# Opening matmuls on zeros in twelve narrow pieces, and key transposes that wait head by head

## The chip, the cores and the metric

The kernel runs on one core of a Trainium2 chip. The metric is the device time of one execution in microseconds; lower is better. A core has TensorE (PE; its weight loads are listed apart as PEld), VectorE (DVE), ScalarE (ACT), GpSimd (POOL) and the queue engine SyncE (SP). They run side by side and wait for each other by semaphores.

## The reference, cut to what matters

One step of a decoder with two layers, for a prompt of 256 tokens and 64 sample tokens (320 columns in all), width 1024. The first layer is retention (projections, a decayed score matrix, a state per head, an output projection), then one shared key and value pair is computed, then a block-sparse attention layer reads it. The changed code touches two things: the very start, and the normalised keys.

```python
def shared_kv(x, kv_norm_w, w_kv, k_norm_w):
    kv = rmsnorm(x, kv_norm_w) @ w_kv
    k, v = jnp.split(kv, 2, axis=-1)
    k = rmsnorm(k.reshape(B, T, MOBA_HEADS, MOBA_HD), k_norm_w)   # per head
    ...
```

The keys leave the kernel as rows (tokens by features), and are used inside it as columns (features by tokens), hence the transposes.

## The kernel before

All work is one hand-written list of steps, `make_schedule()`. Every engine runs through the same list and emits its own share of each step, so the order on each engine is fixed by the list, and semaphores join them. Weights come in chunks of 1 MB. ACT makes a rounded copy `w_hi` (L1239), DVE the remainder `w_lo` (L1579), and PE runs each projection as three matmuls, hi by hi, hi by lo, lo by hi (L940 with 320 moving columns, L937 with 512; the stacked sample tile is L921). A chunk is split in four parts during the chunk before it, at steps `WS`.

**The start.** PE waits for POOL's `eps_done`, then runs three matmuls of zeros (L956, tile `qz`) into bank 7, whose result nobody reads. Then it transposes the norm weights (L959, needed by ACT's `wcols`, L1312) and the inputs block by block (L877): eight blocks of the first 128 tokens, four of the second, four of the samples, and the rest when it has landed. DVE copies banks 0 and 1 to `xT` (L1633), ACT scales the others into `xn_hi` (L1323), DVE makes `xn_lo` (L1628), and the first projection begins.

**The keys.** The keys come in two halves of four heads (`mk` with h = 0 and 1), each in three token tiles in the order samples, first 128, second 128 (`tile_order`: 2, 0, 1). For each tile ACT squares the sums (L1407), DVE reduces and scales (L1737, L1742, L1747), and step `KN` on ACT multiplies the four heads of the tile by their root (L1504, four instructions of 128 columns, each some 0.3 us behind the last). `KN` signals `rows_done` once per tile. Steps `KX` 0 to 3 on PE transpose two heads each: three tiles by two heads is six transposes (L1126), head i into bank 6 + i. ACT then copies the two banks to `mkT` (L1511). `KX` 0 and 2 come first after the last tile of their half, `KX` 1 and 3 follow six projection matmuls later. Behind `KX` 1 six matmuls and then step `KS` 2 follow on PE: 64 calls of narrow key scores (L1111). An f32 matmul call is two matmuls and two weight loads on PE, so this pass is 256 instructions; a transpose is one of each. Also behind it, ACT cannot write the next half's sample rows (L1226) before the rows of the first half are stored (`rows_stored`, issued at L846 on SP) and before PE's tile at L921 is full.

Of the kernel before, what the change touches and what calls it, by code (L numbers as in the profile page):

```python
# [30 lines left out]
ACT = mybir.ActivationFunctionType  # L31
AX = mybir.AxisListType

P = 128
# [112 lines left out]
def tile_order(kind, a, b):  # L147

    return (2, 0, 1) if kind == "mk" or (kind, a, b) == ("mo", 1, 1) else tuple(range(TILES[kind]))
# [171 lines left out]
def build(nc, a):  # L321
# [3 lines left out]
    with ctx:  # L325
# [209 lines left out]
        def await_free(pe, b, *key):  # L535

            if use[(*key, b)]:
                pe.wait_ge(bank_read[b], use[(*key, b)])
# [140 lines left out]
        def _(sp):  # L679
# [77 lines left out]
            for step in steps:  # L757
# [65 lines left out]
                elif kind == "US":  # L823
                    store_pair(4 * step[1] + 3)
                    load_pair(4 * step[1] + 6)
                elif kind == "ME" and 1 <= step[1] < MH - 1:
                    if step[1] == 1:
                        sp.wait_ge(pages_loaded, 16)
                        await_ret_over(sp)
                        sp.dma_start(knw[:, :], bass.AP(a["k_norm_w"].tensor, 0, [[0, P], [1, HD]])).then_inc(knw_loaded, 16)  # L830
                    for n in ((), (0, 1), (2,), (3,), (4,), (5, 6), (7,))[step[1]]:
                        load_page(n)
                elif kind == "KP":
                    for n, at in ORDERED_AT.items():
                        if at == step[1]:
                            load_page(n)
                elif kind == "SE" and step[1] == 1:
                    await_ks(sp, 3)
                    sp.dma_start(tb[:, :, :], bass.AP(scratch.tensor, FAR - P, [[skew, P], [LINE, MH], [1, TP]]))\
                        .then_inc(tb_loaded, 16)  # L840
                elif kind == "KX" and step[1] % 2 == 0:
                    p = step[1] // 2
                    for n, t in enumerate(tile_order("mk", p, 1)):
                        m = TOK[t][1]
                        sp.wait_ge(rows_done, 3 * p + n + 1)
                        sp.dma_start(k_out[t][:, 512 * p:512 * p + 512], rows[0:m, t, :]).then_inc(rows_stored, 16)  # L846
                elif kind == "SN":
                    load_page(16 + NCP - 1)
                elif kind == "PV" and 1 <= step[1] <= 16 - NCP:
                    load_page(15 + NCP + step[1])  # L850
                elif kind == "YA" and step[1] == 0:
                    for t in range(3):
                        await_read(sp, *tile_use("mv", 3 + t))
                    for t, (c0, m) in enumerate(TOK):
                        store(v_out[t], mvp[:, t, :] if t < 2 else mvs[0:TS, :])
                elif kind == "TILE" and chunks[step[1]][0] == "mo":
                    p, t = chunks[step[1]][1], step[2]
                    await_read(sp, *tile_use("mo", 3 * p + t))
                    sp.dma_start(y_out[t][:, 512 * p:512 * p + 512], rows[0:TOK[t][1], t, :]).then_inc(rows_stored, 16)
# [8 lines left out]
        def _(pe):  # L868
            def close(mm, b):
                mm.then_inc(bank_full[b], 1)  # L870
# [80 lines left out]
            for step in steps:  # L951
                kind = step[0]
                if kind == "X":
                    pe.wait_ge(eps_done, 1)
                    for n in range(3):
                        pe.matmul(bank[7][:, 0:TP], qz[:, 0:P], qz[:, 0:TP], start=True, stop=True)  # L956
                    pe.wait_ge(eye_loaded, 16)
                    pe.wait_ge(ret_w_loaded, 16)
                    pe.transpose(bank[3][:, 384:392], wrow[0:8, :], ident[0:8, 0:8]).then_inc(wrow_turned, 1)  # L959
# [158 lines left out]
                        last[3].then_inc(ks_done, 1)  # L1118
                elif kind == "KX":
                    c = step[1]  # L1120
                    pe.wait_ge(rows_done, 3 * (c // 2) + 3)
                    def key_columns(i, t):

                        c0 = TOK[t][0]
                        at = 256 * (c % 2) + P * i
                        return pe.transpose(bank[6 + i][:, c0:c0 + P], rows[:, t, at:at + P], ident)  # L1126

                    if c == 0:
                        pe.wait_ge(pads_cleared, 1)
                    for i in range(2):  # L1130
                        await_free(pe, 6 + i, *step)
                        key_columns(i, 0)
                        key_columns(i, 1)
                    for i in range(2):
                        close(key_columns(i, 2), 6 + i)
                elif kind == "SN":
                    await_free(pe, 4, *step)
                    await_read(pe, 6, "KX", 3)
# [82 lines left out]
        def _(act):  # L1221
# [27 lines left out]
            for step in steps:  # L1249
# [248 lines left out]
                elif kind == "KN":  # L1498
# [2 lines left out]
                    m = TOK[t][1]  # L1501
                    await_read(act, *tile_use("mk", 3 * (n // 3) + t))
                    for d in range(4):
                        ins = act.activation(rows[0:m, t, P * d:P * d + P], rows[0:m, t, P * d:P * d + P], ACT.Copy,  # L1504
                                             scale=kss[0:m, n % 2, d:d + 1])
                    ins.then_inc(rows_done, 1)
                elif kind == "KX":
                    act.wait_ge(kt_done, 6)
                    for i in range(2):
# [60 lines left out]
        def _(dve):  # L1570
# [48 lines left out]
            for step in steps:  # L1619
# [74 lines left out]
                elif kind == "TILE":  # L1694
# [33 lines left out]
                    elif what == "mk":  # L1728
# [4 lines left out]
                            upper_half(rows[0:TS, i, :], b).then_inc(sum_done, 1)  # L1733
                        dve.wait_ge(key_sq_done, nk + 1)
                        if nk >= 2:
                            dve.wait_ge(rows_done, nk - 1)
                        dve.tensor_reduce(kss[0:m, nk % 2, :], key_sq[0:m, :].rearrange("p (h d) -> p h d", d=HD), AX.X, ALU.add)\  # L1737
                            .then_inc(key_sum_done, 1)
                        if h:
# [365 lines left out]
```

## Time and profile before

| what | value |
|---|---|
| time, median of 3 runs | 501.35 us (500.54 to 501.76) |
| the profiled execution, its own time | 499.29 us |
| its span, first to last instruction | 497.4 us |
| PE busy | 489.1 us (98%) |
| weight loads busy | 423.8 us (85%) |
| DVE, ACT, POOL busy | 359.0, 260.7, 96.5 us |

PE is busy almost everywhere, so an instruction more on PE costs its time unless PE would have waited there anyway. A matmul's duration in the trace reaches from its start to the end of its passage, and the next one starts before that; what it costs in a stream is the distance from start to start.

### The profile page before, as it was taken

Reading aid. Unit: us, or ns where it says so; the run is one execution under the profiler, and the core shown is the slowest. Engines: PE = TensorE matmul, PEld = TensorE weight load, DVE = VectorE, ACT = ScalarE, POOL = GpSimd, SP = SyncE. Lnnn points to the kernel's source line nnn. Section 1 sums busy time; section 2 is a strip of 40 time slices with the busy share of each in tenths; the row PEclk is TensorE's granted clock in tenths of the full one; section 3 lists DMA queues with packets and bytes.
Section 4 is the critical chain, followed back from the end, with each engine's and each line's share of the span. In section 5 each row is a group of like instructions: output and inputs, shape, how many; then the busy total and the mean of one; then the engine's idle time right before and its main releaser. Section 6 shows DMA issues by size and latency. Waiting matters only on the chain.

```text
span 497.4 us, 9895 instructions
## 1 busy us (share of the span) xinstructions
PE 489.1 (98%) x3685; PEld 423.8 (85%) x3685; DVE 359.0 (72%) x633; ACT 260.7 (52%) x536; POOL 96.5 (19%) x139
## 2 busy tenths in 40 slices
PE   7999999999999999999999999999989999999997
PEld 6889978899788997799799999987757778999885
DVE  3865539894698829896389987998966764775662
ACT  6735533565417724375454364764737655556630
POOL 0291003720063200920000042446002000000000
PEclk9999999999999999999999999999999999999999
DMA  9993978999899998999956899989798477683211
GB/s 264 368 330 118 278 252 304 371 367 238 266 333 394 261 233 300 348 361 238 261 169 211 294 298 224 280 224 220 239 298 281 154 229 234 232 307 124 86 53 53
DMA packets 86770, 125.54 MB, mean 252 GB/s; under 512 B 5491, under 2 KB 51524, under 8 KB 86596
## 3 DMA queue, kind: packets, MB, share of 16 engines
q1 hardware_dynamic: 85874, 124.63, 80.6%
q8 instruction: 29, 0.48, 0.4%
q0 software_dynamic: 768, 0.28, 0.4%
q14 instruction: 17, 0.14, 0.1%
q10 hardware_dynamic: 82, 0.02, 0.0%
HBM read 98.93 MB, written 27.57 MB: 254 GB/s over the span
## 4 chain that ended last, share of the span: by engine, by line
PE 88%; DVE 3%; DMA 3%; ACT 2%; issue 1%; SPq 1%; DVEq 0%; ACTq 0%
PE bank L940 44%; PE bank L937 18%; PE bank L921 7%; PE bank L1049 3%; DMA w_raw<-in_ret_w_in 3%; PE bank L1169 2%; PE bank L1063 1%; PE bank L996 1%; PE bank L1111 1%; PE bank L1215 1%; ACT rows L1504 1%; DVE small L1737 1%; PE bank L1029 1%; PE bank L1030 1%; PE bank L1031 1%
## 5 line engine op out<-in xcount | busy, mean ns | idle before, releaser
L1579 DVE TENSOR_TENSOR w_lo<-w_raw,w_hi 128x512 fp32r<-128x512 f32 x207 | 145.1, 739 | 62.8 <-ACT w_hi L1239 62.0
L1239 ACT ACTIVATE w_hi<-w_raw 128x512 fp32r<-128x512 f32 x208 | 118.6, 620 | 65.8 <-PE bank L940 35.4
L940 PE MATMUL bank<-xn_hi,w_hi 128*128 128x320 f32 x320 | 100.2, 317 | 0.2 <-DVE raw_qk L1669 0.2
L940 PE MATMUL bank<-xn_hi,w_lo 128*128 128x320 f32 x320 | 97.6, 309 | 0.0
L940 PE MATMUL bank<-xn_lo,w_hi 128*128 128x320 f32 x320 | 97.5, 309 | 0.0
L937 PE MATMUL bank<-w_hi,xn_hi 128*128 128x512 f32 x160 | 64.8, 405 | 0.0
L940 PEld LDWEIGHTS bank<-xn_hi,w_hi 128*128 128x128 f32 x320 | 59.7, 188 | 4.2 <-issue 2.7
L937 PE MATMUL bank<-w_lo,xn_hi 128*128 128x512 f32 x160 | 62.5, 391 | 0.0
L937 PE MATMUL bank<-w_hi,xn_lo 128*128 128x512 f32 x160 | 62.4, 390 | 0.0
L940 PE MATMUL bank<-ym_hi,w_hi 128*128 128x320 f32 x192 | 60.9, 317 | 0.0
L940 PEld LDWEIGHTS bank<-xn_lo,w_hi 128*128 128x128 f32 x320 | 59.8, 188 | 0.2
L940 PEld LDWEIGHTS bank<-xn_hi,w_lo 128*128 128x128 f32 x320 | 59.8, 188 | 0.0
L940 PE MATMUL bank<-ym_hi,w_lo 128*128 128x320 f32 x192 | 59.3, 309 | 0.0
L940 PE MATMUL bank<-ym_lo,w_hi 128*128 128x320 f32 x192 | 59.3, 309 | 0.0
L1798 DVE SCALAR_TENSOR_TENSOR st<-st,bank 128x512 f32<-128x512 f32 x64 | 39.6, 681 | 6.1 <-PE bank L1063 6.1
L2007 POOL TENSOR_TENSOR fin<-raw_qk,cst 128x320 f32<-128x320 f32 x16 | 17.4, 1109 | 109.8 <-DMA out_ret_state_prompt<-fin 101.5
L940 PEld LDWEIGHTS bank<-ym_hi,w_hi 128*128 128x128 f32 x192 | 36.1, 188 | 1.8 <-issue 1.7
L937 PEld LDWEIGHTS bank<-w_hi,xn_hi 128*128 128x128 f32 x160 | 30.0, 188 | 8.6 <-issue 3.1
L940 PEld LDWEIGHTS bank<-ym_lo,w_hi 128*128 128x128 f32 x192 | 36.1, 188 | 0.1
L940 PEld LDWEIGHTS bank<-ym_hi,w_lo 128*128 128x128 f32 x192 | 36.0, 188 | 0.0
L937 PEld LDWEIGHTS bank<-w_lo,xn_hi 128*128 128x128 f32 x160 | 30.0, 188 | 6.6
L937 PEld LDWEIGHTS bank<-w_hi,xn_lo 128*128 128x128 f32 x160 | 30.1, 188 | 5.6
(289 smaller groups left out, 780.1 us busy)
## 6 DMA issues: line engine op xcount, KB each, us to landing
w_raw<-in_ret_w_in SPq DMA_DIRECT2D x23, 1024.0 KB, 11.0
st<-in_state_ret SPq DMA_DIRECT2D x32, 512.0 KB, 8.2
out_ret_state_sample<-st SPq DMA_DIRECT2D x32, 512.0 KB, 4.6
w_raw<-in_ret_w_out SPq DMA_DIRECT2D x8, 1024.0 KB, 8.7
w_raw<-in_moba_w_in SPq DMA_DIRECT2D x8, 1024.0 KB, 6.5
w_raw<-in_w_kv SPq DMA_DIRECT2D x8, 1024.0 KB, 8.1
cache<-in_cache_v SPq DMA_DIRECT2D x16, 512.0 KB, 4.9
cache<-in_cache_k SPq DMA_DIRECT2D x44, 128.0 KB, 4.5
```

What stands on the lines that cost most here:

```text
L921: mm = pe.matmul(bank[b][:, :], xn_hi[:, k, TP:T + TS], w[:, wk, :], start=k == 0 and n == 0, stop=k == KT - 1 and n == 1)
L937: mm = pe.matmul(bank[b][0:m, :], x[:, k, c0:c0 + m], w[:, wk, :], **flags)
L940: mm = pe.matmul(bank[out][:, 0:T], w[:, wk, P * tile:P * tile + P], x[:, k, :], **flags)
L996: mm = pe.matmul(bank[5][0:m, col:col + n], kT[:, d, j:j + m], qT[:, d, i0:i0 + n], start=d == 0, stop=d == 1)
L1029: pe.matmul(bank[3 + d][:, :], kd_hi[:, t, at], vp_hi[:, t, :], start=t == 0, stop=False)
L1030: pe.matmul(bank[3 + d][:, :], kd_hi[:, t, at], vp_lo[:, t, :], start=False, stop=False)
L1049: mm = pe.matmul(bank[5][32 * j:32 * j + 32, :], qz[:, q0:q0 + 32], st[:, b, DV * d:DV * d + DV], start=False, stop=g == 1 and d == 1, ski ...
L1169: mm = pe.matmul(bank[7][32 * j:32 * j + 32, P * u:P * u + P], window(8 * half_at + 4 * (j // 2) + 2 * pg + j % 2, b % 4), page_at(16 + m) ...
L1239: act.activation(w_hi[:, c % 2, part], w_raw[:, c % RAW, part], ACT.Copy).then_inc(w_hi_done, 1)
L1579: dve.tensor_tensor(w_lo[:, c % 2, part], w_raw[:, c % RAW, part], w_hi[:, c % 2, part].bitcast(F32), ALU.subtract).then_inc(w_lo_done, 1)
L1798: dve.scalar_tensor_tensor(state, state, math.exp(NEW * LOG_DECAY[h]), bank[up_bank(b, d)][:, :], ALU.mult, ALU.add).then_inc(bank_read[up ...
L2007: done(pool.tensor_tensor(to, x, tab, ALU.mult))
```

## The change

The opening runs twelve matmuls of 64 columns in place of three of 256. Each call reloads the same 128 columns of weights. `KN` signals each head, so that all counts of `rows_done` are multiplied by four. `KX` takes the tiles in the order in which they become ready, and waits for the last tile head by head. The waits for banks 6 and 7 both stand ahead of the first tile.

```diff
-                    for n in range(3):
-                        pe.matmul(bank[7][:, 0:TP], qz[:, 0:P], qz[:, 0:TP], start=True, stop=True)
+                    for n in range(12):
+                        pe.matmul(bank[7][:, 0:TP // 4], qz[:, 0:P], qz[:, 0:TP // 4], start=True, stop=True)
...
-                    pe.wait_ge(rows_done, 3 * (c // 2) + 3)
...
-                    for i in range(2):
-                        await_free(pe, 6 + i, *step)
-                        key_columns(i, 0)
-                        key_columns(i, 1)
-                    for i in range(2):
-                        close(key_columns(i, 2), 6 + i)
+                    order = tile_order("mk", c // 2, 0)
+                    pe.wait_ge(rows_done, 4 * (3 * (c // 2) + 2))
+                    for n, t in enumerate(order):
+                        for i in range(2):
+                            if n == 0:
+                                await_free(pe, 6 + i, *step)
+                            if n == 2:
+                                pe.wait_ge(rows_done, 4 * (3 * (c // 2) + 2) + 2 * (c % 2) + i + 1)
+                            mm = key_columns(i, t)
+                            if n == 2:
+                                close(mm, 6 + i)
...
-                        ins = act.activation(rows[0:m, t, P * d:P * d + P], rows[0:m, t, P * d:P * d + P], ACT.Copy,
-                                             scale=kss[0:m, n % 2, d:d + 1])
-                    ins.then_inc(rows_done, 1)
+                        act.activation(rows[0:m, t, P * d:P * d + P], rows[0:m, t, P * d:P * d + P], ACT.Copy,
+                                       scale=kss[0:m, n % 2, d:d + 1]).then_inc(rows_done, 1)
```

The waits on `rows_done` of SP (before the stores of the rows) and of DVE (before it reuses `kss`) are multiplied by four likewise and stand for the same tiles.

PE's first rows before the change. `qz` is the tile of zeros, `st` holds the inputs, `fin` the norm weights.

```order
L867 UNCONDITIONAL_BRANCH [waits barrier_Pool_Activation_PE_DVE_SP_release]
L956 MATMUL bank<-qz 128x256 [waits eps_done]
L956 MATMUL bank<-qz 128x256 x2
L959 MATMUL bank<-eye,fin 128x8 [waits ret_w_loaded,eye_loaded]
L877 MATMUL bank<-eye,st 128x128 [waits x_loaded0]
```

The same rows of the changed kernel.

```order
L867 UNCONDITIONAL_BRANCH [waits barrier_Pool_Activation_PE_DVE_SP_release]
L956 MATMUL bank<-qz 128x64 [waits eps_done]
L956 MATMUL bank<-qz 128x64 x11
L959 MATMUL bank<-eye,fin 128x8 [waits ret_w_loaded,eye_loaded]
L877 MATMUL bank<-eye,st 128x128 [waits x_loaded0]
```

Nothing moved there; nine calls came in, which are 36 instructions of PE, and everything behind them stands 36 instructions later in PE's code.

PE's rows at `KX` 0 before the change (the projection of the second half's tile ends above it and goes on below it).

```order
L937 MATMUL bank<-w_lo,xn_hi 128x512
L1126 MATMUL bank<-eye,rows 128x128 [waits bank_read6,pads_cleared,rows_done]
L1126 MATMUL bank<-eye,rows 128x128
L1126 MATMUL bank<-eye,rows 128x128 [waits bank_read7]
L1126 MATMUL bank<-eye,rows 128x128 x3
```

The same place in the changed kernel.

```order
L937 MATMUL bank<-w_lo,xn_hi 128x512
L1125 MATMUL bank<-eye,rows 128x128 [waits bank_read6,rows_done,pads_cleared]
L1125 MATMUL bank<-eye,rows 128x128 [waits bank_read7]
L1125 MATMUL bank<-eye,rows 128x128 x2
L1125 MATMUL bank<-eye,rows 128x128 [waits rows_done] x2
```

The wait for the last tile moved from the first transpose to the fifth and sixth, and the wait for bank 7 from the third to the second. `KX` 1, 2 and 3 changed in the same way.

## Rows read from the trace of the kernel before

**Rows 1.** The page: busy time, granted clock in 40 slices, PE's code queue.
```profile
PE 489.1 (98%) x3685; PEld 423.8 (85%) x3685; DVE 359.0 (72%) x633; ACT 260.7 (52%) x536; POOL 96.5 (19%) x139
...
PEclk9999999999999999999999999999999999999999
...
q8 instruction: 29, 0.48, 0.4%
```

**Rows 2.** Weight loads by line: ns min/median/max, first and last start, forms.
```profile
L956 PEld LDWEIGHTS bank<-qz x6: 285/337/337, 1.7 to 3.5; 128*128 128x128 f32 x6
L877 PEld LDWEIGHTS bank<-eye,st x24: 134/140/230, 4.8 to 10.3; 128*128 128x128 f32 x16, 64*128 64x128 f32 x8
L970 PEld LDWEIGHTS bank<-gs,ones x6: 182/188/192, 18.5 to 19.3; 128*128 128x128 f32 x4, 64*128 64x128 f32 x2
```

**Rows 3.** Timeline of PE, first 20 us: start, us from first to last.
```profile
1.67 2.93 PE L956 MATMUL bank<-qz 128*128 128x256 f32 x6 [1.67 <-POOL eps L1964]
4.58 0.27 PE L959 MATMUL bank<-eye,fin 8*128 8x8 f32 x1
...
5.05 1.27 PE L877 MATMUL bank<-eye,st 128*128 128x128 f32 x5
...
6.54 0.64 PE L877 MATMUL bank<-eye,st 128*128 128x128 f32 x4
...
8.62 0.66 PE L877 MATMUL bank<-eye,st 128*128 128x128 f32 x4 [1.05 <-DMA st<-in_x_prompt]
...
18.66 0.61 PE L970 MATMUL bank<-gs,ones 128*128 128x128 f32 x4
...
19.20 0.43 PE L970 MATMUL bank<-gs,ones 64*128 64x64 f32 x2
```

**Rows 4.** Timeline of ACT and DVE between 7 and 10 us.
```profile
7.86 0.93 ACT L1323 ACTIVATE xn_hi<-bank,wcols 128x320 fp32r<-128x320 f32 x2
...
7.42 0.89 DVE L1633 COPY xT<-bank 128x320 f32<-128x320 f32 x2 [7.42 <-PE bank L877]
8.22 0.68 DVE L1579 TENSOR_TENSOR w_lo<-w_raw,w_hi 128x512 fp32r<-128x512 f32 x1
```

**Rows 5.** Timeline of PE from 21 to 23 us.
```profile
21.65 0.60 PE L1076 MATMUL bank<-fin 32*8 32x264 f32 x2
22.41 0.41 PE L940 MATMUL bank<-xn_hi,w_hi 128*128 128x320 f32 x1 [0.16 <-DVE raw_qk L1669]
```

**Rows 6.** One stretch: length; busy of PE, PEld, DVE, ACT, POOL; clock; DMA; GB/s.
```profile
22.40:355.90 333.50, 333.49 (x2321) 292.90 (x2321) 258.21 (x410) 169.84 (x317) 90.27 (x123) 1.00 0.91 275
```

**Rows 7.** Timeline of PE around the key transposes.
```profile
355.90 0.39 PE L937 MATMUL bank<-w_lo,xn_hi 128*128 128x512 f32 x1
356.56 0.87 PE L1126 MATMUL bank<-eye,rows 128*128 128x128 f32 x6 [0.27 <-ACT rows L1504]
...
358.65 0.82 PE L1126 MATMUL bank<-eye,rows 128*128 128x128 f32 x6
...
380.25 0.87 PE L1126 MATMUL bank<-eye,rows 128*128 128x128 f32 x6
```

**Rows 8.** Timeline of ACT in the same place.
```profile
355.22 1.28 ACT L1504 ACTIVATE rows<-rows,small 128x128 f32<-128x128 f32 x4 [0.51 <-DVE small L1747]
356.41 1.66 ACT L1239 ACTIVATE w_hi<-w_raw 128x512 fp32r<-128x512 f32 x3
357.97 0.74 ACT L1511 ACTIVATE mkT<-bank 128x320 f32<-128x320 f32 x2
```

**Rows 9.** Timeline of PE in the pass of key scores of step KS 2.
```profile
365.08 0.63 PE L1111 MATMUL bank<-scr,wide 32*32 32x256 f32 x8 [1.61 <-issue]
```

**Rows 10.** Stores of the key rows, and the ACT instruction that waits for them.
```profile
360.02 1.06 SPq L846 DMA_DIRECT2D out_k_prompt<-rows  x2
...
DMA to landing us min/median/max: 6.9/7.1/7.3
...
367.99 0.60 ACT L1226 ACTIVATE rows<-bank 64x512 f32<-64x512 f32 x1 [4.16 <-PE bank L921]
```

More of the change, by code:

```diff
@@ L844, in _ @@
                         m = TOK[t][1]
-                        sp.wait_ge(rows_done, 3 * p + n + 1)
+                        sp.wait_ge(rows_done, 4 * (3 * p + n + 1))
                         sp.dma_start(k_out[t][:, 512 * p:512 * p + 512], rows[0:m, t, :]).then_inc(rows_stored, 16)
@@ L1735, in _ @@
                         if nk >= 2:
-                            dve.wait_ge(rows_done, nk - 1)
+                            dve.wait_ge(rows_done, 4 * (nk - 1))
                         dve.tensor_reduce(kss[0:m, nk % 2, :], key_sq[0:m, :].rearrange("p (h d) -> p h d", d=HD), AX.X, ALU.add)\
```

## The prediction

> **What bounds the kernel now.** I read the page first: PE is busy 98% of the span and runs 3685 matmuls with as many weight loads [rows 1]. Then the timeline of PE for its idle times. There are five: before the opening [rows 3], 1.05 us for the inputs [rows 3], 0.16 us at 22.41 [rows 5], 0.27 us before a key transpose [rows 7], and 1.61 us inside a pass of key scores, ended by "issue", that is, by no semaphore [rows 9]. Between 22.4 and 355.9 us PE is never idle [rows 6]. So a delay that reaches 22.4 us arrives whole at 355.9; what happens before can be absorbed only by the waits for the inputs and at 22.41.
>
> **The opening.** Three calls are six matmuls with six weight loads, 2.93 us from the first start to the last end, some 0.43 us from start to start [rows 3]. Twelve calls are 24 of each. Streaming is a quarter of 0.43, 0.107 us a piece, and 24 × 0.107 = 2.6 us, as long as before. That is the lower bound. But each piece loads 128 columns of f32 weights. At the faster clock the trace has such loads with 128 moving columns, (0.61 - 0.275) / 3 = 0.11 us apart, and with 64, two that begin at 19.20 and are through about 0.27 us later, so 0.11 too, after a late first one [rows 3]. Half the columns save nothing: the load sets the pace. The durations say the same: a transpose's load lasts 140 ns, this one 188, and in the opening 337 against 230 at most [rows 2].
>
> The clock: the page prints full clock in every slice [rows 1], but equal transposes stand (1.27 - 0.42) / 4 = 0.21 us apart at 5.05 and (0.64 - 0.31) / 3 = 0.11 from 6.54 on [rows 3]. So PE is at 1.2 GHz until about 6.5 us and at 2.4 GHz after. At the lower level a load-bound piece takes twice 0.11, say 0.213 us. From an effective first start at 1.83, 24 × 0.213 = 5.1 us end at 6.9, not 4.4. Before, PE then stood until 4.58 for its first data [rows 3], and the input transposes ran from 4.84; now they run from 6.96, 2.1 us later.
>
> The Trainium skill ("TensorE: Matmul & The Clock Gate", LDWEIGHTS (loading the stationary operand)) gives a weight load as its columns divided by 1.2, in ns: 107 ns for these 128 columns. By that rule the pieces would stream at 0.107 us and the opening would cost nothing; the rows above, where 64 columns are no faster than 128, speak against it for f32.
>
> How much of 2.1 us is left? From 6.96 on, with the clock up: twelve at 0.109, a break of 0.1, four at about 0.06, done at 8.6 in place of 7.4. Just then the rest of the inputs has landed (8.62), so PE's idle 1.05 us is used up. But DVE's copies start with the sample blocks: 7.42 becomes 8.67; ACT's first scaling 7.86 becomes 8.8 [rows 4]. Behind the copies come DVE's weight split (0.68 us [rows 4]) and the first `xn_lo`, which the first projection's third term needs. It starts at 9.6 and stutters; I get the end of its first six matmuls 1.0 us later than before. From there PE streams without a gap to 21.87, and at 22.41 it had to wait: its last matmul at L1076 is streamed by 21.65 + 2 × 0.22 = 22.09, the next is effective at 22.5, held by DVE's `raw_qk`, which hangs on a weight transfer and not on PE. So 0.4 us are absorbed. Left: **+0.6 us**, taken as it is to 355.9.
>
> **The key transposes.** At KX 0 PE is free at 355.90 + 0.23 = 356.13 and starts effectively at 356.61, when the fourth head of ACT's row is done (355.22 + 1.28 = 356.50) [rows 7, 8]. KX 0 needs heads 0 and 1: at 0.3 us from head to head they are done at about 355.6 and 355.9. In the changed kernel nothing holds it: it ends 0.48 us earlier. But KX 1 needs bank 6 and 7 again, and these are freed by ACT's copies, which stand behind three weight splits: 356.41 to 358.07, then copies ending at about 358.39 and 358.71 [rows 8]. ACT is busy without a gap, so they don't come sooner. KX 1 started at 358.65 and came to its wait for bank 7 two transposes later, 0.05 us after it was free. Now it arrives at 358.17, does one transpose when bank 6 is free, and holds for bank 7 until 358.76: five more at 0.109, next matmul at about 359.37. Before it was 359.30. So the gain of 0.48 is given back wholly and 0.06 more, since the wait for bank 7 stands one transpose earlier. The second half has the same shape: KX 2 gains less, some 0.25 us, since its row names no wait [rows 7], and KX 3 meets the copies behind the same three splits; ends about 0.04 later. **+0.05 us** in all. Four signals in place of one on ACT cost nothing that I see: its instructions with a signal each, as the splits at 0.52 us apart, run gapless [rows 8].
>
> **The 36 instructions.** PE's code comes through a queue of its own: 29 packets, 0.48 MB [rows 1], so 16.5 KB or some 254 of PE's 7370 instructions each. PE is short of code when it runs through one block before the next has come. The pass at KS 2 is 256 instructions in under 3 us, and its stall lies 8 matmuls, 16 instructions, before its end [rows 9]: the block begins 16 before the pass and holds almost nothing but the pass, the worst alignment there is. The other three passes don't stall. Everything now stands 36 later, so the boundary falls 52 before the end of the pass, and the block before it begins near KX 0's first instruction and not within KX 1. The request goes out by about 355.8 and not at 358.65, when KX 1 began [rows 7]; if it takes as long as before (6.4 us, until 365.08), the code is there at 362.2, when it is wanted. The 1.6 us (1.8 with what a stream would have filled) vanish.
>
> The Trainium skill ("Runtime: NRT & Kernel Launch", Instruction fetch mechanics) speaks of blocks of 16 KiB, 256 instructions, whose boundary costs mostly nothing; the block size agrees with the packets, the stall of 1.61 us does not agree with the cost.
>
> What is late next? PE gets 1.8 us ahead, and at L1226 ACT waits for the stored rows of the first half: issued at 360.02 and about 360.6, landed 6.9 to 7.3 us later, so at 367.9; it starts at 367.99 [rows 10]. PE's tile was full at about 367.8, so the row names it, but the store alone holds ACT there. All that follows up to the next 380.21 (rows of the last tile, four heads) runs on ACT and DVE, one behind the other, and PE meets it at KX 2 and, after the splits, at KX 3. What PE is ahead, it waits there. **0 us**, bounds -1.8 (all kept) and +0.
>
> **Sum.** 499.29 + 0.6 + 0.05 + 0 = 499.9 for an execution like the profiled one. That lies 2.1 below the median of the runs shown; on the median, 501.35 + 0.65 = **502.0 us**.
>
> **The rivals.**
> *The clock rises later.* The opening now keeps the array streaming half the time, and what PE did before the rise is only shown for the wide one. If PE is at 1.2 GHz until about 10 us, twelve transposes at 0.213 end at 9.5, the samples at 10.1, the rest at 10.8; DVE's copies come 2.8 us late, and after the 0.4 at 22.4 some +2.3 remain: 503.7. For it: nothing shows the narrow form. Against: PE is not idle in it.
> *The opening costs nothing.* Loads hide behind 64 columns, or the clock is up by 5 us: +0.05, 501.4. Against it stand the L970 rows.
> *Faster: the stall's time is kept.* One mechanism: the rows' stores land before PE's tile is full, so that PE, not the store, releases L1226, and each 0.1 us of PE counts. It decides if they land by 366.2 rather than 367.9: then -1.8 + 0.65, 500.2. For it: the row names PE and the two are 0.15 us apart. Against: the stores' issue hangs on SP's page loads, which the change doesn't touch.
> *Another pass now runs out of code.* Boundaries move in all dense passes; the closest I find has 7 us. Up to +2: 504.
>
> **How the numbers follow.** Chances: forecast 0.50 (its own range 501.4 to 502.8), late clock 0.17, free opening 0.15, stall kept 0.12, new stall 0.06. What a measurement tells from no change is 0.3%, 1.5 us. Faster by more needs the kept stall and a free opening together: 0.05. Slower by more is the late clock (most of it), the new stall and the forecast's edge: 0.18. The rest, 0.77, is within. The range goes from the kept stall to just short of the late clock's centre, 500.2 to 503.4, and leaves out under 0.2.
>
> **What would show it.** L956 as 24 matmuls over about 5 us and the first L877 near 6.8; DVE's L1633 near 8.7; the first L1511 after KX 0 still right behind three splits and KX 1 no earlier than before relative to it; no 1.6 us "issue" at L1111, but waits of PE at L1125 at KX 2 and 3 of about 1 us each; L1226 released by the store. Wrong it is if L956 takes 3 us, if equal transposes stand 0.21 apart beyond 8 us, or if the end of KX 3 moves against L1226.

## The result, and the profile after

| what | before | after |
|---|---|---|
| time, median | 501.14 us of 10 runs (499.80 to 502.49) | 503.40 us of 10 runs (502.58 to 506.23) |
| the profiled execution, its own time | 499.29 us | 502.65 us |
| its span | 497.4 us | 500.7 us |

The ratio is 1.0048, with a 95% interval of 1.0031 to 1.0065. The change makes the kernel slower, by 2.3 us where I had forecast 0.65 us.

From the page of the changed kernel: busy time and instructions, granted clock in 40 slices, the code queue. They answer to [rows 1].

```profile
PE 492.4 (98%) x3703; PEld 427.7 (85%) x3703; DVE 357.5 (71%) x633; ACT 260.3 (52%) x536; POOL 95.2 (19%) x139
...
PEclk9999999999999999999999999999999999999999
...
q8 instruction: 29, 0.48, 0.4%
```

PE has 18 matmuls more, and its busy time grew by 3.3 us, as the span did. The timeline of PE in the first 13 us answers to [rows 3]: start, us from first to last.

```profile
1.68 5.38 PE L956 MATMUL bank<-qz 128*128 128x64 f32 x24 [1.68 <-POOL eps L1967]
6.99 0.27 PE L959 MATMUL bank<-eye,fin 8*128 8x8 f32 x1
7.19 3.93 PE L877 MATMUL bank<-eye,st 128*128 128x128 f32 x20
11.29 0.56 PE L940 MATMUL bank<-xn_hi,w_hi 128*128 128x320 f32 x2 [0.17 <-DVE xT L1636]
```

One stretch of the same engine: us from and to, length, busy (count), clock, DMA share, GB/s.

```profile
7.20:9.40 2.20, 2.20 (x12) 1.00 1.09 294
```

The opening is as long as forecast, and the first input transpose stands at 7.19. But only eleven transposes start in the 2.2 us from there, 0.21 us apart (the row's count of twelve takes in the norm weights' transpose, which still runs at 7.20). PE is still at 1.2 GHz, where I had counted on 2.4 GHz and 0.109 us. The clock column reads 1.00 here as in [rows 1], because the trace's record of the granted clock begins only at 10.29 us; where it begins, the distances change. Before, that record begins at 6.60 us.

The first rows of DVE and ACT that wait for the transposes answer to [rows 4].

```profile
10.35 0.89 DVE L1636 COPY xT<-bank 128x320 f32<-128x320 f32 x2 [10.35 <-PE bank L877]
...
10.51 0.95 ACT L1327 ACTIVATE xn_hi<-bank,wcols 128x320 fp32r<-128x320 f32 x2 [1.91 <-PE bank L877]
```

They are 2.9 and 2.7 us later than before. How much of that stays is read from one and the same instruction further on, ACT's pair of weight splits that starts at 42.74 us in the trace of the kernel before (first row) and at 45.00 in that of the changed one (second).

```profile
42.74 1.14 ACT L1239 ACTIVATE w_hi<-w_raw 128x512 fp32r<-128x512 f32 x2
```

```profile
45.00 1.14 ACT L1243 ACTIVATE w_hi<-w_raw 128x512 fp32r<-128x512 f32 x2
```

So 2.27 us come out of the opening. The waits of PE over the whole span (us in total, times, longest) show what else there is.

```profile
PE bank L1111 <- issue: 1.7, 1, 1.7
PE bank L956 <- POOL eps L1967: 1.7, 1, 1.7
PE bank L1072 <- DVE scr L1818: 1.1, 1, 1.1
PE bank L1125 <- ACT mkT L1514: 0.2, 1, 0.2
PE bank L940 <- DVE xT L1636: 0.2, 1, 0.2
```

The wait for the inputs and that for `raw_qk` [rows 3, 5] are gone, as the prediction had it. A wait of 1.1 us at L1072 near 256 us is new. And the stall at L1111 [rows 9], which was to vanish, is there. Its place moved as forecast, from 8 to 26 matmuls before the end of the pass, which is 52 instructions. The timeline of PE from the key transposes to that stall (answers to [rows 7, 9]):

```profile
359.62 0.81 PE L1125 MATMUL bank<-eye,rows 128*128 128x128 f32 x6
...
362.05 0.99 PE L1125 MATMUL bank<-eye,rows 128*128 128x128 f32 x6 [0.24 <-ACT mkT L1514]
362.80 0.47 PE L937 MATMUL bank<-w_hi,xn_hi 128*128 128x512 f32 x1
...
368.38 0.43 PE L1111 MATMUL bank<-ktc,wide 32*32 32x256 f32 x5 [1.68 <-issue]
```

and ACT's heads of the last tile and the row that waits for the stores, which answer to [rows 8, 10]:

```profile
358.75 1.28 ACT L1508 ACTIVATE rows<-rows,small 128x128 f32<-128x128 f32 x4 [0.51 <-DVE small L1750]
...
371.24 0.59 ACT L1230 ACTIVATE rows<-bank 64x512 f32<-64x512 f32 x1 [4.59 <-PE bank L921]
```

The heads are 3.53 us later than in [rows 8]. Measured from them, KX 0 starts 0.47 us earlier than before, KX 1 has to wait for ACT's copies, and the next projection matmul stands at 362.80 - 3.53 = 359.27. That is 0.05 us later than the same matmul in the trace of the kernel before:

```profile
359.22 0.47 PE L937 MATMUL bank<-w_hi,xn_hi 128*128 128x512 f32 x1
```

### The profile page after: what moved, and what is told of

Its sections match the earlier page's. It is cut to its first block, busy times and chain, and to the rows that moved or that the text cites. A ratio compares the mean times of both kernels' runs of the same rounds, so it can differ in the third digit from the quotient of the medians.

```text
span 500.7 us, 9931 instructions
## 1 busy us (share of the span) xinstructions
PE 492.4 (98%) x3703; PEld 427.7 (85%) x3703; DVE 357.5 (71%) x633; ACT 260.3 (52%) x536; POOL 95.2 (19%) x139
## 4 chain that ended last, share of the span: by engine, by line
PE 83%; DVE 7%; DMA 3%; ACT 3%; SPq 2%; issue 2%; POOL 0%; DVEq 0%; ACTq 0%; POOLq 0%
PE bank L940 41%; PE bank L937 18%; PE bank L921 6%; DMA w_raw<-in_ret_w_out 3%; DVE w_lo L1582 2%; PE bank L1049 2%; PE bank L1111 2%; PE bank L1173 2%; PE bank L1063 1%; PE bank L956 1%; PE bank L996 1%; DVE st L1801 1%; PE bank L1219 1%; ACT w_hi L1243 1%; PE bank L1206 1%
## 5 line engine op out<-in xcount | busy, mean ns | idle before, releaser
L2010 POOL TENSOR_TENSOR fin<-raw_qk,cst 128x320 f32<-128x320 f32 x16 | 15.6, 993 | 105.9 <-DMA out_ret_state_prompt<-fin 98.4
```

What stands on the lines that cost most here:

```text
L2010: done(pool.tensor_tensor(to, x, tab, ALU.mult))
```

## The experiments

One execution is cut into three by two instructions of ACT, the splits at 42.74 us and the four heads at 355.22 us in the trace before. "Start" is how late the first is against 42.74, "middle" what is added until the second, "tail" what is added until the end (the span as printed, less 497.4). "Clock up" is where the record of the granted clock begins; "low later" gives later stretches at 1.2 GHz, start and length, but for the last 3 us. "Turn" is the first input transpose. The kernels named "again" and "third" are the kernel of that name, profiled once more.

```
kernel         profiled turn  clock   start middle tail   low later
               us       at    up at
before         499.29   4.78   6.60    0     0     0
before_again   501.20   4.69   4.57   0.48  0.92  0.41
signals_only   499.88   4.75   7.86  -0.17 -0.07  0.64
order_only     502.89   4.73   5.27   1.18  0.35  1.87   8.7: 3.4; 367.1: 3.4
keys_only      501.35   4.73   7.01   1.90 -0.13  0.33   10.4: 3.4
keys_again     505.63   4.92   6.37   0.90  0.47  4.83   368.2: 6.8
keys_third     503.36   4.73   7.11   0.42  0.10  3.48   368.9: 3.4
open0          504.92   5.26   9.20   0.35  1.13  4.02   367.6: 6.8
open6x64       502.83   4.77  13.77   1.96 -0.01  1.65   368.8: 3.4
open4x256      500.06   5.59   6.41   0.03 -0.09  0.86
open6x256      500.76   6.22   4.97   0.22  0.96  0.22
keys6x256      501.56   6.08   4.67   0.02  0.35  1.92   366.5: 3.4
keys12x128     500.47   6.80   6.11   0.49 -0.03  0.54
open12x128     502.63   7.25   7.04   0.94 -0.12  1.77   382.5: 3.4
open12x64      506.87   7.18  10.75   2.26  0.18  5.06   382.8: 6.8
after          502.65   7.19  10.29   2.27  1.25 -0.22
after_again    503.21   7.19   9.42   1.94 -0.07  1.83   367.8: 3.4
after_third    503.22   7.19  10.44   2.27 -0.13  1.66   368.8: 3.4
before_pad36   502.87   7.76   7.69   1.44  0.25  1.80   383.2: 3.4
keys_pad36     503.25   7.77   8.17   1.63  1.39  0.99
```

Single executions of one kernel differ by up to 5.8 us, so the verdicts stand on the ratios, and the table says where a difference sits.

### The opening alone, and the same length streaming all the time

**open12x64**: the new opening, keys as before.

```diff
-                    for n in range(3):
-                        pe.matmul(bank[7][:, 0:TP], qz[:, 0:P], qz[:, 0:TP], start=True, stop=True)
+                    for n in range(12):
+                        pe.matmul(bank[7][:, 0:TP // 4], qz[:, 0:P], qz[:, 0:TP // 4], start=True, stop=True)
```

> Opening of twelve matmuls of 64 columns alone; keys as before. Late-clock theory: the changed opening keeps PE at 1.2 GHz until about 10.3 us instead of 6.6, the input transposes end 3 us later and about 2.3 us arrive at the end: ratio 1.0045. Rival (the keys or the moved code cost a part): 0.6 to 1.2 us here, ratio 1.001 to 1.0025, and the rest in the run of the keys alone.

Measured: 503.72 us median, ratio 1.0050 (1.0030 to 1.0070), start 2.26 us, clock up at 10.75. The opening alone costs what the whole change costs.

**open12x128**: the same with `TP // 2` in place of `TP // 4`, that is 128 columns in each piece.

> Opening of twelve matmuls of 128 columns, keys as before. As many weight loads and as much code as twelve of 64, and the same 5.1 us long, but each piece streams 128 columns, about as long as its load takes, so that the array streams nearly all the time. Late-clock theory: full clock at about 6.6 us or sooner, input transposes 0.109 us apart, and only the +0.6 us remain that the later start costs (ratio 1.001). Rival (it is the length of the opening, or the 36 instructions, whatever streams in it): as twelve of 64, +2.3 us.

Measured: 502.82 us, ratio 1.0028 (1.0003 to 1.0054). The timeline of PE in its first 10 us, and a stretch from its first input transpose on:

```profile
1.68 5.49 PE L956 MATMUL bank<-qz 128*128 128x128 f32 x24 [1.68 <-POOL eps L1964]
7.10 0.22 PE L959 MATMUL bank<-eye,fin 8*128 8x8 f32 x1
7.25 2.63 PE L877 MATMUL bank<-eye,st 128*128 128x128 f32 x20
```

```profile
7.26:9.35 2.09, 2.04 (x18) 1.00 1.10 256
```

Twice the columns take the same time, so the weight load does set the pace of the narrow piece. But now the clock is up at 7.04, 17 input transposes start in 2.1 us where eleven did in the changed kernel's 2.2, and the start costs 0.94 us and not 2.26. Code and length of the opening are the same in both kernels, so this difference is that of the columns alone. The intervals of the two ratios overlap; the difference of the medians, 0.9 us, has the sign and about the size of the difference at the start, 1.3 us.

**open6x256**: six matmuls of 256 columns (`range(6)`). **open4x256**: four (`range(4)`).

> Opening of six matmuls of 256 columns, keys as before: the same length as twelve of 64 (5.1 us at the lower clock), but half the weight loads and streaming all the time. Late-clock theory: full clock at about 6.6 us, offset at 33 us 0.6 to 0.95 as with twelve of 128, ratio 1.001 to 1.002. Rival (length alone): offset 2.3, ratio 1.0045.

> Opening of four matmuls of 256 columns, keys as before: 8 pieces, 3.4 us at 1.2 GHz, end near 5.2, PE never idle before the inputs' rest. By what six of 256 showed: clock up near 5, offset at 33 us 0 to 0.3, stall at L1111 as before; ratio 0.998 to 1.001. If only a length of 5 us lifts the clock so early: up near 6.6, offset 0.3 to 0.6.

Measured: 501.54 us, ratio 1.0007 (0.9983 to 1.0030), start 0.22; and 501.00 us, ratio 1.0000 (0.9977 to 1.0023), start 0.03. With six, PE in the first 7 us:

```profile
1.67 4.47 PE L956 MATMUL bank<-qz 128*128 128x256 f32 x12 [1.67 <-POOL eps L1964]
6.07 0.22 PE L959 MATMUL bank<-eye,fin 8*128 8x8 f32 x1
6.22 1.92 PE L877 MATMUL bank<-eye,st 128*128 128x128 f32 x16
```

The clock is up at 4.97, within the opening, so that twelve pieces of 0.427 us take 4.47 us and not 5.1, and the real work follows at full clock. Real work that starts 1.4 us later costs nothing that can be measured. The expectation of 6.6 us was wrong, to the kernel's good; with four it came up at 6.41, not near 5.

**open6x64**: `range(6)` and `TP // 4`. **open0**: `range(0)`, no opening matmuls.

> Opening of six matmuls of 64 columns (12 pieces, 2.6 us, end at 4.4 as before), keys as before. The input transposes start on time. Late-clock theory: PE stays at 1.2 GHz until about 8 to 10 us, twelve transposes at 0.213 us end at 7.4 and the samples at 7.9 instead of 7.4, copies 0.5 to 0.8 us late: +0.2 to +1.5 us. Rival (the length of the opening is all): 0, clock up at 6.6.

> No opening matmuls at all, keys as before; PE begins with the norm weights' transpose at about 4.6 us. Late-clock theory: PE stays at 1.2 GHz well beyond 6.6 us; twelve transposes at 0.213 us from 4.84 end at 7.4, the rest of the inputs is turned at 0.213 too: offset at 33 us 0.5 to 2, ratio 1.001 to 1.004. Rival (the opening sets no clock): offset 0.

Measured: 501.33 us, ratio 0.9996 (0.9973 to 1.0019); and 504.73 us, ratio 1.0075 (1.0046 to 1.0104). In both profiles the clock is late (13.77 and 9.20), but the starts differ, 1.96 and 0.35 us. The profile of six narrow matmuls shows that a late clock can cost much at the start even when the transposes begin on time; the ratio of its twelve executions shows no cost. How late the clock is in those was not recorded, so what a late clock costs behind a short opening stays open. open0 loses in its tail, where the stall at L1111 is 2.9 us long and the clock falls behind it.

Now take the profiles in which the first transpose stands beyond 6 us, in the order of their clock (7.69 and 8.17 are the two kernels with padding, further down, whose transposes also begin 0.5 to 1.7 us later than in the others):

```
clock up at    4.67  4.97  6.11  7.04  7.69  8.17  9.42  10.29 10.44 10.75
start, us      0.02  0.22  0.49  0.94  1.44  1.63  1.94  2.27  2.27  2.26
```

With the opening of before the start hangs on something else: the landing of the rest of the inputs, whose first transpose stands at 8.57 to 9.54 us in the seven profiles. Their starts go from -0.17 to 1.90 us, and the two largest, 1.18 and 1.90, are those in which the clock fell once more behind the wait for the inputs ("low later" at 8.7 and 10.4).

### The keys

**keys_only**, **keys_again**, **keys_third**: the key part of the change as in its diff, opening as before.

> Key transposes and signals changed alone; opening of three matmuls of 256 columns as before. My step in the prediction: +0.05 us, ratio 1.000, with the gain of 0.48 us at KX 0 given back at KX 1. Rival (the keys cost part of the 2.3): +0.5 to +1.5 us, ratio 1.001 to 1.003.

> The keys alone, timed again, since the first time of it (median 504.6, granted clock 0.990 to 0.993 in most executions) stood against its own profile (501.35). If the key change is worth nothing by itself, and its executions met more falls of the clock by chance: ratio 0.998 to 1.002, clock 1.0 in some executions as in the kernel before. Rival (the key change brings the falls of the clock): ratio 1.004 or more again.

> The key change alone, looked at a third time. If it costs by a late code block: a stall of 2 us or more at L1111 and a clock of 1.2 GHz for 3.4 or 6.8 us right behind it, and no other loss between 34 us and the end but the chance wait at L1072. If the stall is 1.8 us as in the kernel before and the time 501 us, the cost is that the long stall is more frequent, not that it is always there.

Measured: 504.61 us, ratio 1.0051 (1.0021 to 1.0082); again 504.08 us, ratio 1.0047 (1.0021 to 1.0072); the single third execution 503.36 us. I had expected nothing, and the keys alone cost 2.4 to 2.5 us by the ratios. In two of the three profiles the tail is long (4.83 and 3.48 us). PE's waits in the third:

```profile
PE bank L1111 <- issue: 3.8, 1, 3.8
PE bank L956 <- POOL eps L1967: 1.7, 1, 1.7
```

and in the second (keys_again) PE behind the stall, then three stretches around it (columns as above):

```profile
368.65 1.08 PE L1111 MATMUL bank<-scr,wide 32*32 32x256 f32 x8 [3.74 <-issue]
369.66 0.80 PE L921 MATMUL bank<-w_hi,xn_hi 128*128 128x512 f32 x1
370.25 0.63 PE L921 MATMUL bank<-w_lo,xn_hi 128*128 128x512 f32 x1
370.68 0.63 PE L921 MATMUL bank<-w_hi,xn_hi 128*128 128x512 f32 x1
```

```profile
356.00:364.00 8.00, 7.78 (x132) 1.00 0.89 262
364.00:368.00 4.00, 0.91 (x46) 1.00 1.03 310
368.00:375.00 7.00, 6.35 (x21) 0.51 0.78 296
```

The stall is 3.7 us long, twice that of [rows 9], and right behind it PE runs at half its clock for 6.8 us: matmuls stand 0.43 us apart that stood 0.23 apart. On the page this is one digit (before, every slice has a 9, [rows 1]):

```profile
PEclk9999999999999999999999999999979999999999
```

**signals_only**: `KN` signals each head, waits times four, transposes as before. **order_only**: signals as before, and in `KX`

```diff
-                    for i in range(2):
-                        await_free(pe, 6 + i, *step)
-                        key_columns(i, 0)
-                        key_columns(i, 1)
-                    for i in range(2):
-                        close(key_columns(i, 2), 6 + i)
+                    for n, t in enumerate(tile_order("mk", c // 2, 0)):
+                        for i in range(2):
+                            if n == 0:
+                                await_free(pe, 6 + i, *step)
+                            mm = key_columns(i, t)
+                            if n == 2:
+                                close(mm, 6 + i)
```

> Only the signals: KN counts rows_done once per head in place of once per tile, all waits times four, key transposes and opening as before. If the keys' +2.7 us come from the signals: ratio 1.004 or more. If they come from the order and the earlier start of the transposes, or from chance: 0.999 to 1.001.

> Only the order of the key transposes and the place of the waits for banks 6 and 7; the wait for all rows of the half stays ahead of them, signals and opening as before. By my step: KX 1 and KX 3 hold one transpose earlier for bank 7, +0.05 us, ratio 1.000. If the keys' +2.7 us come from this order: 1.003 or more.

Measured: 501.14 us, ratio 0.9994 (0.9972 to 1.0017); and 501.80 us, ratio 1.0006 (0.9980 to 1.0033). Neither costs. What is left is that the transposes no longer wait for all heads, or that it takes the three together: signals and order in one kernel, with the wait kept, were not run. It shows as a longer stall in two profiles of three; in the first, with a stall of 1.6 us, the tail is 0.33 us. The mean granted clock of the 20 timed executions of the keys alone says the same: it is 0.993 or less in ten of them, and in 5 of 31 and 0 of 25 of the kernel before beside them. That is not all of it: the five executions of the keys alone with a clock of 0.999 or more have a median of 502.65 us, still 2 us above such executions of the kernel before.

### Both, with an opening that streams

**keys6x256** is the changed kernel with six matmuls of 256 columns, **keys12x128** with twelve of 128.

> The key change with an opening of six matmuls of 256 columns. That opening alone was +0.2 us at 33 us, and its 12 instructions took the stall at L1111 away in its profile. If the keys cost by the stall (a late code block, 1.7 to 3.9 us, with a fall of the clock behind it) and the 12 instructions take it away here too: ratio 1.000 to 1.002. If the code block is as late with the key change as in all four of its profiles so far, or the cost lies elsewhere: 1.004 to 1.006.

> The changed kernel with 128 moving columns in each opening matmul in place of 64: same code, same length of the opening (5.1 us), streaming all the time. If the late clock is the cause: clock up by about 7, offset at 33 us 0.9 and not 2.3, ratio 1.001 to 1.003 (some 1 to 1.5 us faster than the changed kernel). If the code block and what is behind it is the cause: 1.0045 again.

Measured: 501.23 us, ratio 1.0003 (0.9977 to 1.0029); and 501.95 us, ratio 1.0028 (1.0006 to 1.0050). With 256 columns the loss is gone. With 128, and the code in exactly the same place as in the changed kernel, 1.0 us of 2.4 is given back, and the start is 0.49 us; again the intervals overlap.

Two pairs of kernels now differ in the columns alone, 64 against 128, with and without the keys. Taken together, each execution scaled by its own kernel before, the narrow ones are 1.1 us slower on the mean of 22 against 24 executions (95% interval 0.4 to 1.8, by drawing the executions anew). So the columns are clear of the noise, and they are about half of the 2.3 us. The rest came in with the twelve calls whatever their columns: openings of twelve pieces of 128 are both at 1.0028, six of 256 at 1.0007 and 1.0003. The twelve begin real work 0.6 to 1.2 us later than the six and are 24 instructions of PE longer; no run separates these.

A fall of the clock late in the kernel hides much of this in single executions. One of 3.4 us takes the mean granted clock of an execution to 0.997 (half of 3.4 in 500 us). Those at 0.999 or more have none:

```
opening                     executions   median, us
before (3 of 256)               81         500.5
6 of 256, with and without keys 14         500.7
12 of 128, likewise              9         501.6
12 of 64, likewise              11         502.9
```

The key change adds nothing in any of the four pairs with another opening: 1.0048 against 1.0050 without it, 1.0028 against 1.0028, 1.0003 against 1.0007, and with the padding below 1.0066 against 1.0073. It costs with the opening of before alone. The stall at L1111 is there in both kernels of this section (2.1 and 1.6 us).

### The place of the code alone

**before_pad36** and **keys_pad36**: 36 instructions of PE that only test a semaphore already at its value, ahead of the opening of before.

```diff
+                    for n in range(72):
+                        pe.wait_ge(eps_done, 0)
                     pe.wait_ge(eps_done, 1)
```

> The kernel before with the same 36 empty instructions ahead of the opening. My step on the 36 instructions: the stall at L1111 vanishes, and the rows' store and KX 2 and 3 take it back, 0 us, ratio 0.999 to 1.001; bound if all is kept -1.8 us, 0.996. In the profile no issue wait at L1111, and a wait of about 2 us at L1126.

> The key change with the opening of before, and 36 empty instructions of PE ahead of the opening, where PE waits anyway, so that its code stands as in the changed kernel. If the +2.3 us are the opening: ratio 0.999 to 1.001. If they come from the key change with this position of the code: 1.004 or more.

Measured: 504.79 us, ratio 1.0073 (1.0051 to 1.0095); and 503.75 us, ratio 1.0066 (1.0039 to 1.0094). The 36 were meant to be free and weren't: the opening starts 3 us later.

```profile
4.73 2.90 PE L958 MATMUL bank<-qz 128*128 128x256 f32 x6 [4.73 <-issue]
7.56 0.27 PE L961 MATMUL bank<-eye,fin 8*128 8x8 f32 x1
```

So the ratios say nothing of the position alone. The profile of before_pad36 does show what the prediction had said of it. PE's waits:

```profile
PE bank L958 <- issue: 4.7, 1, 4.7
PE bank L1128 <- ACT rows L1506: 2.4, 2, 2.1
PE bank L940 <- DVE xT L1635: 0.2, 1, 0.2
```

No stall at L1111, and 2.1 us of waiting at KX 2 in its place. The same stands in open12x128 (2.1 us at L1126) and open6x256. But behind such a wait the clock fell too (383.2 and 382.5 in the table; in open6x256 it didn't), so the wait that came in its place can bring a loss of its own.

### The two kernels, profiled again

**before_again**, **after_again**, **after_third**: the two kernels themselves.

> The kernel before, looked at once more. Its first profile had 499.29 us against a median of 501.1 to 501.5. If the difference lies in what varies from one execution to the next (the inputs' landing near 8.6 us, the stall at L1111 and a fall of the clock behind it), some of it shows here: offset at 33 us between 0 and 1, stall between 1.7 and 4 us, and a clock at 1.2 GHz for 3.4 us behind it if the stall is above 2 us.

> The changed kernel itself, looked at once more. If the late clock (about 10.3 us) comes from the half-streaming opening, it is late again and the weight splits stand 2.27 us later from 30 us on. The 1.2 us that PE waited at L1072 near 256 us in the first profile followed a slow pair of transfers: if that is chance, the offset at 350 us is 2.3 to 2.8 now and not 3.5. The stall at L1111 depends on when the code block's transfer starts after PE has entered the block before (6.3 us in the first profile, 2.4 and 4.1 in the two openings without key change, where it was gone): under about 5.5 us no stall, else one of up to 1.8 us.

> The changed kernel, third look. Late-clock theory: clock up between 9 and 11 us, offset at 33 us 1.9 to 2.3. Late block: if the key change is what delays it, the stall at L1111 is there again, 1.7 us or more; if the two stalls seen were chance, it is gone as in the openings of twelve without the key change.

Measured: 501.20, 503.21 and 503.22 us. With the narrow opening of twelve the start is 1.94 to 2.27 us in four profiles of four, 2.2 on the mean. With the opening of before and code in its place it is 0.67 us on the mean of seven (before, before_again, signals_only, order_only and the three of the keys alone, whose change comes only at 350 us). The difference is 1.5 us. The middle is chance: 1.25, -0.07 and -0.13 after, and from -0.13 to 0.92 in the seven. Where it is largest, it is the wait at L1072: in the first trace after, ACT's splits of the chunk before it, which the transfer of `w_out` releases, start 4.48 us later than before (246.67 and 242.19), though PE was only 2.27 us late. The tail is -0.22, 1.83 and 1.66 after (1.09 on the mean) against 0.73 in the four without the new waits for single heads. That adds up to 1.5 + 0.1 + 0.35 = 2.0 us, where the medians have 2.3; with so few profiles the parts are known to some tenths of a microsecond at best.

## Why the prediction was wrong, step by step

**The length of the opening: right.** The load sets the pace of the narrow pieces. 24 pieces stand 0.213 us apart, and 128 columns in a piece are no slower than 64. The Trainium skill's rule ("TensorE: Matmul & The Clock Gate", LDWEIGHTS (loading the stationary operand)), columns divided by 1.2 in ns, would have made them 0.107 us; for f32 operands the measured piece is twice that at 1.2 GHz.

**The clock in it: the step that failed.** I wrote "From 6.96 on, with the clock up". The first transpose did stand at 7.19, but the clock came up at 9.4 to 10.4. The term was put at +0.6 us and measured 1.5 on the means (2.27 against the one profiled execution before). That is 0.9 of the 1.6 us by which the sum fell short of the measured change; the two pairs of kernels that differ in the columns alone put the price of the narrow pieces at 1.1 us. It was mis-sized because I carried the moment of 6.5 us over from an opening of wide pieces to one of narrow ones. With pieces of 128 columns, whose clock was up at 6.1 and 7.0, the start is 0.5 and 0.9 us, as I had worked out against the same execution. Against the mean of the seven it is near nothing, while those two kernels lose 1.4 us by their ratios. Where the rest of that lies, no profile shows. My rival of the late clock named the mechanism, "keeps the array streaming half the time", and came near in value, 503.7 (measured 503.4), and I gave it 0.17. The value is partly luck: its +2.3 us is what one pair of profiles shows, the means give 1.5, and other parts made up the rest. Against it I had only that PE is not idle in the narrow opening. Idle it wasn't (one row of 5.38 us), and the clock was late all the same, in three profiles of the changed kernel and one of open12x64, while the opening of 128 columns, as long and as full of loads, had it at 6.1 and 7.0.

**0.4 us absorbed at 22.41: right in kind.** 2.93 us at DVE's copy become 2.27 at 42.74, and the wait for `raw_qk` is gone.

**The keys, +0.05 us: right where I looked, wrong in the whole.** KX 0 gains 0.47 (forecast 0.48), KX 1 gives it back, the next matmul moves by 0.05 (forecast 0.06). In the changed kernel the keys add nothing that the ratios show. But alone they cost 2.5 us, which my step can't give, and why only with the opening of before stays open.

**The 36 instructions, 0 us: half right.** I said that the request for the code block goes out earlier, the stall vanishes, and PE waits at KX 2 and 3 for what it gained. With the keys untouched the stall was gone in three profiles of three (open12x64, open12x128, before_pad36), and PE waited near KX 2 instead. With the new keys and the same 36 it was gone in keys_pad36 but not in keys12x128 (1.6 us), and in the changed kernel the block was late all the same: the stall was 1.7, 2.2 and 2.2 us. By the trace's record of the code queue, with the lateness of ACT's four heads taken off, the transfer of that block began at 362.0 to 362.9 us in twelve profiles, with code moved by 0, 4, 12 or 36 instructions; at 359.0 to 360.7 in the five without a stall, all moved by 12 or 36; at 363.9 in open0, moved by -12; and at 364.7 in keys_again and keys_third. I had taken only the request into account, and the start of the transfer did not follow it. The DMA engines are taken up almost wholly then (0.89 and 1.03 in the DMA column of the stretches above). Why, with the new keys, an earlier request mostly brings no earlier transfer is not settled: no run here separates it.

The Trainium skill ("Runtime: NRT & Kernel Launch", Instruction fetch mechanics) holds a block's boundary to cost mostly nothing. Here PE stood still for 1.6 to 3.8 us at one boundary in 15 of 20 profiles; its code comes in 29 blocks.

**The size of the noise.** The profiled execution before was 1.9 us below its median. I shifted the sum to the median, which was right, but took the start's cost from the one execution. In six more profiles with the same opening the start came out from 0.17 us earlier to 1.90 us later.

## What to carry to other kernels

The moment at which the clock came up was measured for the old opening: when its pieces change, price the first real work at both levels, and read from the distance of equal matmuls, not from the clock column or the busy time, where the rise lies. If an opening is to be longer, lengthen it with wide matmuls: real work 1.4 us later behind six wide ones cost nothing here, and 2.4 us later behind twelve narrow ones 1.5 us at the start. In a dense pass, look at where a code block ends; a stall there costs again when the clock falls behind it, and changes that seem free can lengthen it. And profile the kernel before more than once: with one and the same opening, the start varied by 2 us.

## What the runs showed that I had not expected

- Behind long idle times of PE late in the kernel the granted clock fell for 3.41 or 6.83 us, 1.7 or 3.4 us of lost work. It fell behind all seven stalls at L1111 that lasted 2.1 to 3.8 us by the waits' rows, and behind one of the eight of 1.6 to 1.9 us (open6x64, 1.9); behind two of the three waits of 2.1 us at KX 2; and in open12x64 behind waits of 0.8, 1.9 and 1.2 us in a row. Within one kernel, the mean granted clock accounts for about half of the variance of the times (0.46, over 291 executions).
- PE resumed 1.3 to 1.6 us after the code block's transfer had ended, in all 15 stalls.
- The same opening of three matmuls of 256 columns saw the clock come up at 4.57, 5.27, 6.37, 6.60, 7.01, 7.11 and 7.86 us.
- 36 instructions that only test a semaphore delayed PE's start from 1.67 to 4.73 us. That is between 0.085 (3.06 / 36) and 0.13 us each (4.73 / 36), though nothing had to be waited for.
